# A hybrid decoder layer on one core: new head ends in the HGRN2 recurrence, wider level products, router weights side by side, the first token tile normed ahead

## What is computed

```
q = silu(hq); f = lb + (1 - lb) * sigmoid(hf); k = 1 - f
b = cumsum(log f) within a chunk
inter     = (q * exp(b)) @ state
att[t,s]  = sum_k q[t,k] * exp(b[t,k] - b[s,k]) * k[s,k]     for s <= t
intra     = att @ v
state     = exp(b_last) * state + (k * exp(b_last - b))^T @ v
```

```
o      = o * rsqrt(mean(o*o) + eps) * hgrn_out_g * silu(hg)
x      = x + concat(norm(attn), o) @ w_out + b_out
logits = rmsnorm(x) @ router_w + router_b         top 4, softmax over them
```

## Time and profile before

| | us |
|---|---|
| median of 3 runs | 2455.72 (2454.97 to 2459.82) |
| the profiled execution | 2460.58, its span 2459.0 |
| PE busy in the span | 2213.6 (90%) |
| DVE busy | 1597.7 (65%) |
| ACT busy | 1352.4 (55%) |
| POOL busy | 474.6 (19%) |

### The profile page before, as it was taken

The page is one execution under the profiler, slowest core; times in us unless marked ns, Lnnn a source line. Parts: engine busy times, 40 slices in busy tenths (PEclk is TensorE's granted clock), DMA queues, the critical chain, the costliest instruction groups (busy, mean ns, idle before and its releaser), DMA issues. The chain is left out here.

```text
span 2459.0 us, 38622 instructions
## 1 busy us (share of the span) xinstructions
PE 2213.6 (90%) x10494; PEld 1838.7 (75%) x10495; DVE 1597.7 (65%) x2261; ACT 1352.4 (55%) x2036; POOL 474.6 (19%) x478
## 2 busy tenths in 40 slices
PE   5999886876993999999999999999999999999992
PEld 4888775876783787877877878777877878778781
DVE  4121167775554777767777676778778677776874
ACT  5211245333231766767666576667667576675764
POOL 3000000321023112113121131213121131121320
PEclk9999978666995999999999999999999999999996
DMA  5111100000333879889798897989798797987976
GB/s 175 39 43 52 69 18 10 9 9 28 117 102 133 280 221 321 263 264 307 226 318 262 263 308 223 318 266 348 233 307 280 245 322 232 303 282 236 326 236 238
DMA packets 260585, 506.15 MB, mean 206 GB/s; under 512 B 34281, under 2 KB 35306, under 8 KB 260368
## 3 DMA queue, kind: packets, MB, share of 16 engines
q1 hardware_dynamic: 241874, 456.02, 55.1%
q0 software_dynamic: 18656, 49.45, 8.6%
q10 hardware_dynamic: 4, 0.02, 0.0%
HBM read 466.24 MB, written 39.17 MB: 206 GB/s over the span
## 5 line engine op out<-in xcount | busy, mean ns | idle before, releaser
L1611 DVE TENSOR_TENSOR wlo<-raw,whi 128x1024 fp32r<-128x1024 f32 x774 | 927.4, 1217 | 110.6 <-ACT whi L1110 92.3
L1110 ACT ACTIVATE whi<-raw 128x1024 fp32r<-128x1024 f32 x775 | 807.0, 1057 | 220.5 <-PE ps L881 125.6
L551 PE MATMUL ps<-whi,xTh 128*128 128x512 f32 x1024 | 405.7, 396 | 0.0
L552 PE MATMUL ps<-wlo,xTh 128*128 128x512 f32 x1024 | 400.8, 391 | 0.0
L553 PE MATMUL ps<-whi,xTl 128*128 128x512 f32 x1024 | 400.5, 391 | 0.0
L1851 POOL DMA_INDIRECT acc_d<-y,icur x64 | 114.3, 1786 | 1031.8 <-ACT y L1152 1022.1
L551 PE MATMUL ps<-whi,aTh 128*128 128x512 f32 x512 | 214.7, 419 | 24.1 <-DVE aTl L1655 24.1
L553 PEld LDWEIGHTS ps<-whi,xTl 128*128 128x128 f32 x1024 | 192.8, 188 | 41.3
L552 PEld LDWEIGHTS ps<-wlo,xTh 128*128 128x128 f32 x1024 | 193.1, 189 | 40.0
L551 PEld LDWEIGHTS ps<-whi,xTh 128*128 128x128 f32 x1024 | 193.1, 189 | 38.7
L553 PE MATMUL ps<-whi,aTl 128*128 128x512 f32 x512 | 202.0, 394 | 0.0
(11 more groups left out here) (285 smaller groups left out, 3983.7 us busy)
## 6 DMA issues: line engine op xcount, KB each, us to landing
raw<-in_w SPq DMA_DIRECT2D x776, 512.0 KB, 6.9
raw<-in_w_in SPq DMA_DIRECT2D x16, 512.0 KB, 3.7
xs<-in_x SPq DMA_DIRECT2D x8, 512.0 KB, 6.1
raw<-in_w_out SPq DMA_DIRECT2D x8, 512.0 KB, 3.7
mix<-in_x SPq DMA_DIRECT2D x8, 512.0 KB, 4.1
acc_d<-mix SPq DMA_DIRECT2D x8, 512.0 KB
h_d<-h SPq DMA_DIRECT2D x8, 512.0 KB
mix<-acc_d SPq DMA_DIRECT2D x8, 512.0 KB, 6.6
```

The lines of the kernel that those rows point to most:

```text
L551: pe.matmul(o, sh, mh_, start=start, stop=False, skip_group_check=skip)
L552: pe.matmul(o, sh, ml_, start=False, stop=False, skip_group_check=skip)
L1110: act.activation(slot(whis, s), slot(raws, s), ACT.Copy).then_inc(split_hi, 1)
L1611: dve.tensor_tensor(slot(wlos, s), slot(raws, s), slot(whis, s).bitcast(F32), ALU.subtract).then_inc(split_lo, 1)
```

## The change

- GpSimd's part of the recurrence goes; VectorE makes the key products too, and counts both by one semaphore.
- Step 7's difference is no longer made by VectorE: ScalarE makes exp(b_last - b) by eight activations, one for a tile, with scale -1 and a bias column.
- A level multiplies `hp` by all of its 128 columns; banks 0 and 1 take even levels, 2 and 3 odd ones and the state matmuls, 4 and 5 transposes and outputs, 6 and 7 the diagonal. The masked copy reads every second run of h columns.
- `hpx` is a buffer of its own for q * exp(b); it lies where g2row comes later, so g2row's load moves behind the recurrence.
- TensorE's order at a head end: transposes and state matmuls of a head, diagonal and level 0 of the next, then the outputs of the first.
- ScalarE copies outputs and squares one level later.
- The first token tile is squared and rooted alone; tiles 1 to 3 are squared next, tiles 4 to 7 and the other roots behind the first two high copies.
- Router weights lie as `rwc` [high, low] side by side: a tile's logits are 8 matmuls of 64 columns and 8 of 32, and `choose` adds the two halves.

```diff
+    hpx = at("hpx", A + 52 * KB, [P, T])
-    rwh = at("rwh", B2 + KB, [P, KT, NE], F32R)
-    rwl = at("rwl", B2 + 2 * KB, [P, KT, NE], F32R)
+    rwc = at("rwc", B2 + KB, [P, KT, 2, NE], F32R)
...
+        def used_by(s):
+            hd, L = divmod(s, STEPS)
+            if L == 0 and hd > 0:
+                return s
+            if L == LEVELS + 1 and hd < HH - 1:
+                return s + 2
+            return s + 1
...
@@ block.sync @@
-            sp.dma_start(g2row[:, :], norm2_g.broadcast_to([P, D])).then_inc(late_in, 16)
...
             sp.wait_ge(rec_out, 2 * HH)
+            sp.dma_start(g2row[:, :], norm2_g.broadcast_to([P, D])).then_inc(late_in, 16)
             sp.dma_start(rw[:, :, :], router_w[0].rearrange("(k p) e -> p k e", p=P)).then_inc(late_in, 16)
...
@@ block.tensor @@
+            def diagonal(hd):
                 if hd == 0:
                     pe.wait_ge(keys_set, HH)
                 else:
-                    pe.wait_ge(rec_out, 2 * hd)
+                    pe.wait_ge(level_copied, LEVELS * (hd - 1) + 1)
...
+            def level(hd, L):
+                s = STEPS * hd + L
+                lev = LEVELS * hd + L
+                pe.wait_ge(prod_dve, dve_prods_by(s))
+                if L >= 2:
+                    pe.wait_ge(level_copied, lev - 1)
+                elif hd > 0 and L == 0:
+                    pe.wait_ge(level_copied, lev)
+                elif hd > 0:
+                    pe.wait_ge(states_set, hd)
+                for t in range(NT):
+                    v = hp[:, s % 2, t * P:(t + 1) * P]
+                    m = pe.matmul(ps[:, 2 * (L % 2) + t // 4, (t % 4) * P:(t % 4 + 1) * P], v, v,
+                                  start=True, stop=True)
+                m.then_inc(level_used, 1)
+            def states(hd):
...
+            def outputs(hd):
...
+            diagonal(0)
+            level(0, 0)
+            for hd in range(HH):
+                if hd > 0:
+                    outputs(hd - 1)
+                for L in range(1, LEVELS):
+                    level(hd, L)
+                states(hd)
+                if hd + 1 < HH:
+                    diagonal(hd + 1)
+                    level(hd + 1, 0)
+            outputs(HH - 1)
...
                 for k in range(KT):
-                    m = mm3(ps[:, 7, 0:NE], h2Th[:, k, :], h2Tl[:, k, :], rwh[:, k, :], rwl[:, k, :],
-                            k == 0, k == KT - 1)
+                    pe.matmul(ps[:, 7, 0:2 * NE], h2Th[:, k, :], rwc[:, k, :, :].rearrange("p a e -> p (a e)"),
+                              start=k == 0, stop=False, skip_group_check=True)
+                    m = pe.matmul(ps[:, 7, 0:NE], h2Tl[:, k, :], rwc[:, k, 0, :], start=False, stop=k == KT - 1,
+                                  skip_group_check=True)
...
@@ block.scalar @@
+                elif L == LEVELS:
+                    act.wait_ge(prod_dve, dve_prods_by(s - 2))
+                    for t in range(NT):
+                        m = act.activation(he[:, s % 2, t * P:(t + 1) * P], hf[:, hd, t * P:(t + 1) * P], ACT.Exp,
+                                           scale=-1.0, bias=hf[:, hd, t * P + P - 1:t * P + P])
+                    m.then_inc(exp_set, 1)
...
-            for t in range(NT):
+            square(0, HH, junks[:, :])
+            act.wait_ge(msq, squares[0])
+            root(rsa[:, 0, 0:1], ssa[:, 0, 0:1], ATTN_W)
+            root(rsa[:, 0, 1:], ssa[:, 0, 1:], P)
+            for t in range(1, 4):
                 square(t, HH, junks[:, :])
-            act.wait_ge(msq, 5 * NT)
-            root(rsa[:, :, 0], ssa[:, :, 0], ATTN_W)
-            root(rsa[:, :, 1:], ssa[:, :, 1:], P)
-            split(7, 3)
...
             mix_hi(0, 0)
             mix_hi(0, 1)
+            for t in range(4, NT):
+                square(t, HH, junks[:, :])
+            act.wait_ge(msq, 5 * NT)
+            root(rsa[:, 1:, 0], ssa[:, 1:, 0], ATTN_W)
+            root(rsa[:, 1:, 1:], ssa[:, 1:, 1:], P)
+            split(7, 3)
...
@@ block.vector @@
-                elif L == LEVELS:
-                    bv, ev = (z.rearrange("p (t n) -> p t n", n=P) for z in (b, e))
-                    dve.tensor_tensor(ev, bv[:, :, P - 1:P].broadcast_to([P, NT, P]), bv, ALU.subtract).then_inc(arg_set, 1)
             def prods(s):
                 hd, L = divmod(s, STEPS)
                 dve.wait_ge(exp_set, s + 1)
-                if s >= 2:
-                    dve.wait_ge(level_used, s - 1)
+                was = s - (STEPS if L == LEVELS + 1 else 4 if L == 1 else 2)
+                if was >= 0:
+                    dve.wait_ge(level_used, used_by(was))
...
-                    dve.tensor_tensor(ov, qv, ev, ALU.mult).then_inc(prod_dve, 1)
+                    dve.tensor_tensor(ov, qv, ev, ALU.mult)
+                    ov, kv, ev = (z.rearrange("p (m two h) -> p m two h", two=2, h=h)[:, :, 0, :]
+                                  for z in (hp[:, s % 2, :], hk[:, hd, :], he[:, s % 2, :]))
+                    dve.tensor_tensor(ov, kv, ev, ALU.mult).then_inc(prod_dve, 1)
...
-                        ps[:, lev % 2, :].rearrange("p (t m h) -> p t m h", t=NT, h=h)))
+                        ps[:, 2 * (L % 2):2 * (L % 2) + 2, :].rearrange(
+                            "p a (t m two h) -> p (a t) m two h", t=4, two=2, h=h)[:, :, :, 1, :]))
...
                 link(dve.tensor_tensor(logit[:, :], ps[:, 7, 0:NE], rb[:, :], ALU.add))
+                link(dve.tensor_tensor(logit[:, :], ps[:, 7, NE:2 * NE], logit[:, :], ALU.add))
...
             mix_lo(0, 1)
+            invert(rsa[:, 1:, :], NT + 4)
             norm(1)
...
@@ block.gpsimd @@
-            for s in range(STEPS * HH):
...
-                    pool.tensor_tensor(o, k, e, ALU.mult).then_inc(prod_pool, 1)
-                elif L == LEVELS:
-                    pool.tensor_tensor(hp[:, s % 2, :], hk[:, hd, :], he[:, s % 2, :], ALU.mult).then_inc(prod_pool, 1)
```

More of the change, by code:

```diff
@@ L671, in _ @@
             pe.wait_ge(heads_out, 2 * NT)
-            for hd in range(HH):
+            def diagonal(hd):
                 if hd == 0:
@@ L682, in _ @@
                 m.then_inc(diag_done, 1)
-                for L in range(LEVELS):
-                    s = STEPS * hd + L
-                    lev = LEVELS * hd + L
-                    h = 64 >> L
-                    pe.wait_ge(prod_dve, dve_prods_by(s))
-                    pe.wait_ge(prod_pool, pool_prods_by(s))
-                    if lev >= 2:
-                        pe.wait_ge(level_copied, lev - 1)
-                    for t in range(NT):
-                        v = hp[:, s % 2, t * P:(t + 1) * P]
-                        m = pe.matmul(ps[:, lev % 2, t * 64:(t + 1) * 64], v,
-                                      v.rearrange("p (m two h) -> p m two h", two=2, h=h)[:, :, 1, :],
-                                      start=True, stop=True)
-                    m.then_inc(level_used, 1)
+            def level(hd, L):
[14 more added lines that the diff above has]
+            def states(hd):
                 s = STEPS * hd + LEVELS
-                pe.wait_ge(prod_pool, pool_prods_by(s))
+                pe.wait_ge(prod_dve, dve_prods_by(s))
                 if hd > 0:
-                    pe.wait_ge(kbT_set, 2 * hd)
+                    pe.wait_ge(rec_out, 2 * hd)
                 for t in range(NT):
@@ L706, in _ @@
                 pe.wait_ge(kbT_set, 2 * hd + 2)
-                if hd > 0:
-                    pe.wait_ge(states_set, hd)
+                pe.wait_ge(level_copied, LEVELS * hd + 6)
                 for t in range(NT - 1):
-                    m = pe.matmul(ps[:, 6 + t // 4, (t % 4) * P:(t % 4 + 1) * P], kbT[:, t, :],
+                    m = pe.matmul(ps[:, 2 + t // 4, (t % 4) * P:(t % 4 + 1) * P], kbT[:, t, :],
                                   hv[:, t, hd * P:(hd + 1) * P], start=True, stop=True)
                 m.then_inc(added_state, 1)
+            def outputs(hd):
                 s = STEPS * hd + LEVELS + 1
@@ L722, in _ @@
                     if t > 0:
-                        m = pe.matmul(o, hp[:, s % 2, t * P:(t + 1) * P], state[:, t - 1, :],
+                        m = pe.matmul(o, hpx[:, t * P:(t + 1) * P], state[:, t - 1, :],
                                       start=False, stop=True)
                 m.then_inc(level_used, 1)
+            diagonal(0)
[10 more added lines that the diff above has]
+            outputs(HH - 1)
             pe.wait_ge(rec_out, 2 * HH)
@@ L1043, in _ @@
                                        ACT.Copy).then_inc(kbT_set, 1)
-                if L == 1 and hd > 0:
+                if L == 2 and hd > 0:
                     outs(hd - 1)
                     act.wait_ge(rec_out, 2 * hd)
-                if 2 <= L < 6 and hd > 0:
-                    for t in range(2 * L - 4, 2 * L - 2):
+                if 3 <= L < 7 and hd > 0:
+                    for t in range(2 * L - 6, 2 * L - 4):
                         square(t, hd, junks[:, :])
@@ L1441, in copies @@
                     if hd > 0:
```

(6 more changed lines are left out.)

55 lines of the change are left out of this document (22 added, 33 removed).

## The result

The changed kernel took 2400.6 us, the median of 4 runs (2396.7 to 2405.3), where the kernel before took 2456.9 in 4 runs beside it: a ratio of 0.977, with a 95% interval of 0.975 to 0.979. It is 56 us faster, where 43.5 were forecast; 2400.6 lies just under the low end of the range, 2402. Run again at two later times, with the kernel before beside it, it was 2401.4 beside 2455.5 (0.978, 0.976 to 0.980) and 2406.1 beside 2455.8 (0.979, 0.978 to 0.981). So the gain is 50 to 56 us, and the first comparison lies at its upper end.

The account below looks back on a forecast made before the run. It took TensorE at a low clock, with VectorE close behind, to bound the recurrence. 33 (recurrence) + 3 (first tile) + 7.5 (router) = 43.5 us off 2455.7 gave 2412 us, range 2402 to 2434.

Parts of the forecast that it names:

- I take 1 us a head: 33 less: Recurrence: TensorE's clock may fall back now and then, costing 1 us a head, so 33 us less.
- 37 less: Recurrence: 135 us against 172 with the high clock throughout, 37 us less.
- rival 2: Recurrence: high clock throughout and head ends fully hidden, 37 + 10.5 us less, 2408 us; chance 0.12.
- The sum's pieces: Recurrence: 24 us to head 0's level 6 products, 3 x 31.7 for heads, 2 for ScalarE, tail 14; 135 in all.
- the stretched difference: Recurrence levels: VectorE's first difference takes 1.50 us while GpSimd multiplies, 0.69 with GpSimd idle; it was to go.
- the wait on hp: Head ends: VectorE's level 1 product stands still 4.0 us until the last output matmul has left hp; it was to go.
- rival 4: Recurrence: strided copies out of PSUM dear, VectorE 3 to 4 us more a head, 2428 us; chance 0.13.
- rival 5: Recurrence levels: slower, a wide record costs its columns; at 0.44 us a record +88 us, 2533 us; chance 0.03.
- rival 3: Recurrence: TensorE stays at the low clock and binds at 40.6 us a head, 2440 us; chance 0.10.
- First tile: Between recurrence and projection: one square instead of eight ahead of the table load, 3 us less (1 to 4).
- router: Projection and router: 16 records a tile instead of 24, with one more VectorE addition, 7.5 us less (5 to 9).

Follow-up runs that it names:

- before_plus_two: The kernel before with two small dead operations more on VectorE behind the recurrence: 2453.9 us, ratio 0.999 to the kernel before.
- recurrence_only: The changed kernel with the router and the first token tile as before, only the recurrence new: 2416.9 us, ratio 0.984 to the kernel before.
- router_undone: The changed kernel with the router as before: 2416.1 us, ratio 0.984 to the kernel before.

## Why the prediction was right or wrong

The direction and the mechanism held; the forecast of the gain was too small by 4 to 5 us in one term, and some 5 us more come from stages that I took as unchanged.

- **The step that failed: "I take 1 us a head: 33 less".** The recurrence fell by 37.9 us (171.9 to 134.0; 37.5 by the means of three profiles each, before_plus_two being the third of before). That is the working of 37 less, 135 us, without the 4 us that I put on for a falling clock. The clock did fall, to 0.66 in one 5-us window at a head end, and VectorE had slack there: a head took 31.45 us, no more than the sum at the high clock, so at the inner head ends the term is nothing. Of sustained levels I had only narrow ones to read, and the sum at the high clock was given to rival 2; its 2408 was nearer than the forecast's 2412.
- The sum's pieces: head 0 to its level-6 products 23.0 us for 24; three heads 31.45 us each for 31.7 and 0.7 for ScalarE; the end 16.6 for 14, where the last outputs ran at 0.69. 23.0 + 94.4 + 16.6 = 134.0.
- The undoings sum to 11.5 (narrow levels) + 16.4 (head ends) + 5.4 (GpSimd's level products) + 3.7 (step 7's difference) = 37.0 of the 37.9. Each was taken back alone from the changed kernel; no run has two of them or adds one to the kernel before, and none gives GpSimd its product of step 7 back, so the near match does not show that they are independent. I had named the stretched difference and the wait on hp; I had not seen that the buffer alone removes nothing and the order alone only part, nor that GpSimd's part is the smaller one.
- Copies with a strided source: 724 ns as before; rival 4 and its 12 us fall. Wide records cost nothing more, rival 5 falls (its sum was off too: 112 records of a head at 0.44 in place of 0.2185 us are 25 us a head, which gives about 2539 and not 2533; and the working of VectorE's level before, 1.4 + 3 x 0.61 - 0.1 + 0.93, is 4.1 and not 3.9; the forecast hangs on neither). TensorE's clock rose and rival 3 falls.
- First tile 3.3 for 3, router 7.2 by the stages of recurrence_only and router_undone for 7.5: both right. The projection stage of the kernel before lay 1 us higher in the first profile than in the second.
- **The range's low end.** 37.5 + 3.3 + 7.2 = 48.0, that is 2407.7 from the 2455.7 that I started from, inside the range. All 14 runs of the changed kernel average 2402.5. Of the 5 us between, up to 4 may be the job loop's shift through VectorE's place (1.9 in the direct trial, not told from zero), and the first comparison's 2400.6 has chance on top; what the rest is stays open. My range had no term for code that I left alone; that, with the 4 us of the clock, is why it missed, and only by 1.4 us.

## What to carry to other kernels

Where narrow float32 matmuls run back to back at a clock of 0.50, try the same products with wider moving sides into spare PSUM columns, and read the granted clock by windows: it can matter more than the wasted columns. Read a head or loop end as a chain over engines, and change order and buffer together: here the buffer alone only moved the wait to the next line, and the order alone took off half. Allow some microseconds either way for stages whose code is untouched, and compare stages, not medians, when a part is worth less than 5 us.

## What had not been expected of the hardware

- Products of the same number of records with 64 moving columns ran at 0.50 through 25 us in which TensorE was busy 24.9; with 128 columns they held 1.00 at 17.4 busy us of 25, while VectorE set the pace.
- GpSimd and VectorE side by side: 28 products moved to GpSimd left VectorE's busy time where it was (118.7 us against 116.9), each of its first differences stretched from 0.69 to 1.22 us.
- Two or three instructions more on VectorE, ahead of a loop, brought GpSimd's copies of 2.31 us inside the loop from 16 of 32 passes to 2. In all 620 passes of the 20 profiles, GpSimd's scatter took 2.30 us or more exactly where a VectorE subtraction had started at least 0.05 us ahead of it, and 1.49 or less elsewhere.
